# Group norm of a Mamba-2 branch on one core: sums in four column strips, roots as rows, spread through DRAM

## The reference

```
def grouped_rmsnorm(y, g, n_groups):
    shp = y.shape
    yf = y.astype(jnp.float32).reshape(*shp[:-1], n_groups, shp[-1] // n_groups)
    yf = yf * lax.rsqrt(jnp.mean(yf * yf, axis=-1, keepdims=True) + EPS)
    return yf.reshape(shp) * g
...
    y = y.reshape(bsz, seqlen, SSD_D_INNER) * jax.nn.silu(z.astype(jnp.float32))
    return grouped_rmsnorm(y, norm_g, SSD_N_GROUPS).astype(z.dtype)
```

## Time and profile before

| | us |
|---|---|
| median of 3 runs | 1487.44 (1487.26 to 1487.52) |
| the profiled execution, its own time | 1488.37 |
| span in the profile | 1486.5 |
| PE busy | 1476.8 (99%) |
| POOL busy | 948.5 (64%) |
| DVE busy | 780.4 (52%) |
| ACT busy | 522.8 (35%) |

### The profile page before, as it was taken

The page is one execution under the profiler, slowest core; times in us unless marked ns, Lnnn a source line. Parts: engine busy times, 40 slices in busy tenths (PEclk is TensorE's granted clock), DMA queues, the critical chain, the costliest instruction groups (busy, mean ns, idle before and its releaser), DMA issues.

```text
span 1486.5 us, 22863 instructions
## 1 busy us (share of the span) xinstructions
PE 1476.8 (99%) x8090; PEld 1211.9 (82%) x8090; DVE 780.4 (52%) x1084; ACT 522.8 (35%) x935; POOL 948.5 (64%) x945
## 2 busy tenths in 40 slices
PE   9999999999999999999999999999999999999999
PEld 7788878888787888888988888888888888888887
DVE  3556675566566648322655545500276483745723
ACT  4481551362263121111622222200242554636441
POOL 5356657665765789898167777799326564655544
PEclk9999999999999999999999999999999999999999
DMA  9244433533633344635022223234223222221231
GB/s 378 84 137 135 135 100 127 170 113 113 191 106 113 113 142 157 131 124 193 21 89 95 99 99 99 99 128 142 71 96 130 80 75 71 71 76 65 77 122 71
DMA packets 67982, 172.31 MB, mean 116 GB/s; under 512 B 7728, under 2 KB 24496, under 8 KB 66384
## 3 DMA queue, kind: packets, MB, share of 16 engines
q1 hardware_dynamic: 45504, 150.05, 30.5%
q10 hardware_dynamic: 22416, 21.44, 4.7%
HBM read 167.20 MB, written 4.27 MB: 115 GB/s over the span
## 4 chain that ended last, share of the span: by engine, by line
PE 97%; DVE 1%; DMA 1%; ACT 1%; issue 0%; SPq 0%; DVEq 0%; ACTq 0%
PE ps L611 17%; PE ps L614 17%; PE ps L613 17%; PE ps L628 6%; PE ps L630 5%; PE ps L629 5%; PE ps L978 4%; PE ps L979 4%; PE ps L977 4%; PE ps L879 1%; PE ps L1165 1%; PE ps L1240 1%; PE ps L1241 1%; PE ps L1242 1%; PE ps L1004 1%; PE ps L1000 1%
## 5 line engine op out<-in xcount | busy, mean ns | idle before, releaser
L561 POOL TENSOR_SCALAR w_hi<-raw 128x512 fp32r<-128x512 f32 x386 | 257.4, 685 | 506.3 <-PE ps L614 243.2
L566 POOL TENSOR_TENSOR w_lo<-raw,w_hi 128x512 fp32r<-128x512 f32 x386 | 527.5, 1388 | 0.0
L611 PE MATMUL ps<-h_hi,w_hi 128*128 128x512 f32 x880 | 347.7, 395 | 0.4 <-ACT zs L1386 0.2
L614 PE MATMUL ps<-h_hi,w_lo 128*128 128x512 f32 x880 | 342.9, 390 | 0.0
L613 PE MATMUL ps<-h_lo,w_hi 128*128 128x512 f32 x880 | 342.8, 390 | 0.0
L611 PEld LDWEIGHTS ps<-h_hi,w_hi 128*128 128x128 f32 x880 | 165.2, 188 | 39.2 <-issue 6.1
L614 PEld LDWEIGHTS ps<-h_hi,w_lo 128*128 128x128 f32 x880 | 165.2, 188 | 34.9
L613 PEld LDWEIGHTS ps<-h_lo,w_hi 128*128 128x128 f32 x880 | 165.3, 188 | 34.3 <-issue 1.0
L628 PE MATMUL ps<-h_hi,w_hi 128*128 128x512 f32 x352 | 140.8, 400 | 0.0
L630 PE MATMUL ps<-h_hi,w_lo 128*128 128x512 f32 x352 | 137.4, 390 | 0.0
L629 PE MATMUL ps<-h_lo,w_hi 128*128 128x512 f32 x352 | 137.3, 390 | 0.0
(11 more groups left out here) (429 smaller groups left out, 2826.4 us busy)
## 6 DMA issues: line engine op xcount, KB each, us to landing
raw<-stream SPq DMA_DIRECT2D x231, 512.0 KB, 3.3
ada_raw<-ada SPq DMA_DIRECT2D x64, 256.0 KB, 3.6
ada<-ada_first SPq DMA_DIRECT2D x8, 1024.0 KB, 14.7
abc<-acs_dram ACTq DMA_DIRECT2D x16, 512.0 KB, 7.2
raw<-stream SPq DMA_DIRECT2D x8, 256.0 KB, 11.9
xr<-x_classes ACTq DMA_DIRECT2D x1, 2048.0 KB, 10.1
x_dram<-xr ACTq DMA_DIRECT2D x1, 2048.0 KB, 8.3
x_res<-x_dram ACTq DMA_DIRECT2D x2, 1024.0 KB, 8.5
```

Of the source, the lines that this page charges most:

```text
L561: nc.gpsimd.tensor_scalar(hi[:, w], raw[:, raw_slot, w], 1.0, 1.0, ALU.mult, ALU.mult).then_inc(split_hi, 1)
L566: ins = nc.gpsimd.tensor_tensor(lo[:, w], raw[:, raw_slot, w], hi[:, w].bitcast(F32), ALU.subtract)
L611: nc.tensor.matmul(ps[:, bank], hi[:, w], x_hi[:, k0 + k], start=start and k == 0, stop=False)
L614: mm = nc.tensor.matmul(ps[:, bank], lo[:, w], x_hi[:, k0 + k], start=False, stop=stop and k == tiles - 1)
```

## The change

The factor of each token takes another way. The sums come out as rows: four products with 32 columns of ones as the weights and 128 tokens of `sct` as the moving side, each into its own strip of 32 partitions of bank 4. ACT takes the root of 128 x 128 (each strip holds 32 equal rows) into a new tile `norm_rows`, now ahead of conv_silu(0); DVE inverts all of it. ACT then sends rows 0, 32, 64 and 96 to a DRAM tensor, waits until they have landed, and reads the 512 numbers back into `sct` on all partitions. DVE's `scale_y` waits for that and reads `sct` in place of the bank. The diagonals and the product with ones are gone, with the semaphores that went with them; `gate_steps` counts 15 steps a group in place of 16.

```diff
+        norm_rows = at("norm_rows", FREE + 138 * KB + 384, [P, P])
...
+        norm_dram = nc.dram_tensor("norm_dram", (NT, P), F32, kind="Internal").ap()
...
             def column_sums(g):
 
-                pe.wait_ge(gate_steps, 1 + 16 * g + 6)
+                pe.wait_ge(gate_steps, 1 + 15 * g + 6)
                 for c in range(NT):
-                    mm = nc.tensor.matmul(ps[:, 4, c:c + 1], sct[:, c * P:(c + 1) * P], ones[:, 0:1], start=True,
-                                          stop=True)
-                mm.then_inc(group_sum, 1)
-
-            def spread_roots(g):
-
-                pe.wait_ge(gate_steps, 1 + 16 * g + 8)
-                nc.tensor.matmul(ps[:, 4], ones[:], sct[:], start=True, stop=True).then_inc(group_sum, 1)
+                    mm = nc.tensor.matmul(ps[32 * c:32 * c + 32, 4, 0:P], ones[:, 0:32], sct[:, c * P:(c + 1) * P],
+                                          start=True, stop=True, skip_group_check=True)
+                mm.then_inc(norm_steps, 1)
...
                 bias_in(1)
+                if not first:
+                    roots(g - 1)
                 conv_silu(0)
                 if not first:
-                    roots(g - 1)
+                    spread_roots(g - 1)
                 bias_in(2)
...
             def roots(g):
-                act.wait_ge(group_sum, 2 * g + 1)
-                A(small[:, 8:12], ps[:, 4, 0:4], ACT.Sqrt, bias=eps[:, 0:1], scale=1.0 / S).then_inc(group_root, 1)
+                act.wait_ge(norm_steps, 2 * g + 1)
+                A(norm_rows[:], ps[:, 4, 0:P], ACT.Sqrt, bias=eps[:, 0:1], scale=1.0 / S).then_inc(norm_steps, 1)
+
+            def spread_roots(g):
+                act.wait_ge(gate_steps, 1 + 15 * g + 7)
+                act.dma_start(norm_dram, norm_rows[0:P:32]).then_inc(norm_moved, 16)
+                act.wait_ge(norm_moved, 32 * g + 16)
+                act.dma_start(sct[:], norm_dram.rearrange("c t -> (c t)").unsqueeze(0).broadcast_to([P, S])
+                              ).then_inc(norm_moved, 16)
...
                 if part == (0, 1):
                     roots(GROUPS - 1)
+                    spread_roots(GROUPS - 1)
...
             def invert_roots(g):
-                dve.wait_ge(group_root, 1 + g + 1)
-                V.reciprocal(small[:, 12:16], small[:, 8:12]).then_inc(gate_steps, 1)
-                dve.wait_ge(gate_steps, 1 + 16 * g + 7)
-                TT(sct[:].rearrange("p (c t) -> p c t", c=NT), ident.unsqueeze(1).broadcast_to([P, NT, P]),
-                   small[:, 12:16].unsqueeze(2).broadcast_to([P, NT, P]), ALU.mult).then_inc(gate_steps, 1)
+                dve.wait_ge(norm_steps, 2 * g + 2)
+                V.reciprocal(norm_rows[:], norm_rows[:]).then_inc(gate_steps, 1)
 
             def scale_y(g):
-                dve.wait_ge(group_sum, 2 * g + 2)
+                dve.wait_ge(norm_moved, 32 * g + 32)
                 for b in range(4):
-                    STT(yg[:, b], yg[:, b], col("ssd_g", 4 * g + b), ps[:, 4], ALU.mult,
+                    STT(yg[:, b], yg[:, b], col("ssd_g", 4 * g + b), sct[:], ALU.mult,
                         ALU.mult).then_inc(gate_steps, 1)
```

More of the change, by code:

```diff
@@ L337, in build @@
         y_squared = sem("y_squared")
-        group_sum = sem("group_sum")
-        group_root = sem("group_root")
+        norm_steps = sem("norm_steps")
+        norm_moved = sem("norm_moved")
         y_hi_ready = sem("y_hi_ready")
@@ L401, in build @@
         out_stored = sem("out_stored")
-        start_at_one = [group_root, chunk_steps, state_steps, mod_ready, gate_steps, biased,
+        start_at_one = [chunk_steps, state_steps, mod_ready, gate_steps, biased,
                         pt_ready, decays, sc_steps, y_done, mix_steps, attended, ada_steps, units_done,
@@ L771, in column_sums @@
             def column_sums(g):
-                pe.wait_ge(gate_steps, 1 + 16 * g + 6)
+                pe.wait_ge(gate_steps, 1 + 15 * g + 6)
                 for c in range(NT):
-                    mm = nc.tensor.matmul(ps[:, 4, c:c + 1], sct[:, c * P:(c + 1) * P], ones[:, 0:1], start=True,
-                                          stop=True)
-                mm.then_inc(group_sum, 1)
-            def spread_roots(g):
-                pe.wait_ge(gate_steps, 1 + 16 * g + 8)
-                nc.tensor.matmul(ps[:, 4], ones[:], sct[:], start=True, stop=True).then_inc(group_sum, 1)
+                    mm = nc.tensor.matmul(ps[32 * c:32 * c + 32, 4, 0:P], ones[:, 0:32], sct[:, c * P:(c + 1) * P],
+                                          start=True, stop=True, skip_group_check=True)
+                mm.then_inc(norm_steps, 1)
             def y_half(u, slot, n, g, bank, free):
                 if n == 0:
-                    pe.wait_ge(gate_steps, 1 + 16 * g + 16)
+                    pe.wait_ge(gate_steps, 1 + 15 * g + 15)
                 unit(u, slot, bank, free, y_hi, y_lo, tiles=4, at_k=4 * (n % 2),
@@ L851, in turn @@
                         pe.wait_ge(dt_tokens, 1)
-                        pe.wait_ge(gate_steps, 1 + 16 * g)
+                        pe.wait_ge(gate_steps, 1 + 15 * g)
                     cols = slice(c * P, (c + 1) * P)
@@ L871, in outputs @@
                     pe.wait_ge(chunk_steps, 1 + 24 * g + 6 * c + 6)
-                    pe.wait_ge(gate_steps, 1 + 16 * g + max(c - 1, 0))
+                    pe.wait_ge(gate_steps, 1 + 15 * g + max(c - 1, 0))
                     if c:
@@ L892, in group @@
                     conv(2)
-                    spread_roots(g - 1)
                     conv(3)
@@ L943, in _ @@
                     column_sums(GROUPS - 1)
-                if i == 3:
-                    spread_roots(GROUPS - 1)
                 if i == 19:
@@ L1371, in conv_silu @@
                     if j == 2 and not first:
-                        act.wait_ge(gate_steps, 16 * g - 9)
+                        act.wait_ge(gate_steps, 15 * g - 8)
                     dst = (BT[:], CT[:])[j] if j < 2 else xcT[:, j - 2]
@@ L1377, in skips @@
                     act.wait_ge(conv_out, 6 * g + 6)
-                    act.wait_ge(gate_steps, 1 + 16 * g)
+                    act.wait_ge(gate_steps, 1 + 15 * g)
                     for b in range(4):
@@ L1407, in square @@
                 def square():
-                    act.wait_ge(gate_steps, 1 + 16 * g + 5)
+                    act.wait_ge(gate_steps, 1 + 15 * g + 5)
                     A(xcT[:], yg[:], ACT.Square).then_inc(y_squared, 1)
@@ L1479, in roots @@
             def roots(g):
-                act.wait_ge(group_sum, 2 * g + 1)
-                A(small[:, 8:12], ps[:, 4, 0:4], ACT.Sqrt, bias=eps[:, 0:1], scale=1.0 / S).then_inc(group_root, 1)
+                act.wait_ge(norm_steps, 2 * g + 1)
[6 more added lines that the diff above has]
+                              ).then_inc(norm_moved, 16)
             def y_his(g, bs):
                 for b in bs:
-                    act.wait_ge(gate_steps, 1 + 16 * g + 8 + b + 1)
+                    act.wait_ge(gate_steps, 1 + 15 * g + 7 + b + 1)
                     A(y_hi[:, b], yg[:, b], ACT.Copy).then_inc(y_hi_ready, 1)
@@ L1982, in gate @@
                 def gate():
-                    dve.wait_ge(gate_steps, 1 + 16 * g + 4)
+                    dve.wait_ge(gate_steps, 1 + 15 * g + 4)
                     dve.wait_ge(evacuated, E_GRP + 6 * g + 4)
```

## The result

The changed kernel takes **1503.41 us** (median of 4 runs, 1503.16 to 1504.39), the kernel before beside it 1487.48. The ratio is 1.0108, with a 95% interval of 1.0096 to 1.0119: slower by 15.9 us, where 1482.6 was forecast and 1481.8 to 1486.6 given as the range. The profiled execution took 1504.39 us with a span of 1502.6.

The account below looks back on a forecast made before the run. PE was taken to bound the touched part; its gain of 1.22 us per group, four times, gave 4.9 us with no new waits, so span 1481.6 and median 1482.6 us, range 1481.8 to 1486.6.

Parts of the forecast that it names:

- PE's part: Column sums and dropped product with ones on PE: gain of 1.22 us per group, four times, 4.9 us.
- The write: ACT's 2 KB write to DRAM in the first loop pass: 1.7 us to landing, 2.7 from above, ACT standing still.
- The read: 256 KB read back into sct in the first loop pass: 4.0 us, between 2.7 and 5.1.
- the page: Trainium skill's DMA rule, about 2.0 us plus bytes over 436 GB/s per transfer: 4.6 us for write and read.
- The start of scale_y: DVE in the first loop pass: scale_y starts at 160.0 instead of 159.48, as the read lands.
- the cover: Slack before PE waits at y(0): ends when scale_y starts at about 160.5, write and read together over 6.25 us.
- The price of meeting POOL: scale_y in the first loop pass: little slowdown beside POOL's one-operand passes, 0.82 us a pass; through by 162.9.
- rival 4: DVE and POOL shut each other out, 1.95 us a pass; last group 2.5 us late, 1485.1 us; chance 0.02.
- deadline: First loop pass: taps(3) with two y_lo must start by 164.1 for PE not to wait at y(0).
- The last group: Behind the loop: scale_y ends at 541.9, y_lo at 547.4, y projections start at 549.5, 2.1 us to spare.
- Rival 1: Round trip late in the loop: PE waits 3.3 us at y(0) in three passes, 1493.7 us; chance 0.08.
- Rival 2: Write and read take 6.4 to 7 us: 0.2 to 1.5 us a pass, 1483.2 to 1487.1 us; chance 0.14.

Follow-up runs that it names:

- PE's part alone: The changed kernel without the two transfers and their waits, and with scale_y reading PSUM bank 4 instead of sct: 1482.65 us.
- PE kept busy: The changed kernel with sixteen unread 128-column products into a free bank ahead of y(0) in each loop pass: 1497.66 us.

## Why the prediction was wrong, point by point

- **PE's part: right.** The last product ahead of the sums starts at 148.66, the second one behind them at 149.67: two beats and 0.56 us; 0.55 was said. PE's part alone gave 5.1 us, for 4.9.

```profile
148.97 0.43 PE L778 MATMUL ps<-sct,ones 128*32 128x128 f32 x8
```

- **The write: too short in the loop.** From issue to the read's issue it is 2.73 us (153.68 to 156.41), 2.82 and 2.66 in the other passes, where 1.7 was taken, the row of a 64 KB store. The bound from above, 2.7, was the value. In the last group the same write takes 1.61, so there 1.7 was right. The stretches of the first write and of the last differ in what else the DMA engines do, a busy share of 0.78 and of 0.04 (last column but one):

```profile
153.70:156.40 2.70, 2.70 (x14) 2.23 (x13) 0.52 (x1) 0.01 (x1) 1.24 (x3) 1.00 0.78 240
547.90:549.50 1.60, 1.60 (x8) 1.32 (x8) 1.60 (x1) 0.00 (x0) 0.47 (x1) 1.00 0.04 12
```

  That other traffic makes the write longer fits this; no run tests it by itself.
- **The read: too long.** With SyncE issuing, it goes out at 155.90 and scale_y starts on its landing at 159.18: 3.3 us at most (3.4 and 3.5 in the other passes), where 4.0 was taken. The pair takes 6.0 to 6.3 us for 5.7, so the sum of the two was nearly right, and nearer than the 4.6 us estimated from the page; what did harm in the change as it stood was their split, since the write's share is the time for which ACT stands.
- **The start of scale_y: late by 0.9 us.** The stop put bias_in(2) at 157.15, taps(2) at 158.09 and scale_y at 160.55. This pass began 0.38 us earlier than in the old trace (ACT's first table load at 143.84 for 144.22), so on the prediction's footing it is 160.9, past the 160.5 at which the text said the cover ends. The text held the late bias_in(2) to be harmless for PE's sake, and carried it to taps(2) at 157.4 (158.5 measured, on that footing).
- **The price of meeting POOL: the step that failed.** The text took 0.82 us for a DVE pass beside POOL's one-operand passes and a mean of 1.38 beside the rest, so that at most one pass in four would suffer: 2.9 us for scale_y, where 4.47 were measured (5.58 and 4.48 in the other passes). One by one, the passes read:

```profile
160.55 0.74 DVE L1904 SCALAR_TENSOR_TENSOR yg<-yg,tab,sct 128x512 f32<-128x512 f32 x1
160.60 1.17 POOL L564 TENSOR_SCALAR w_hi<-raw 128x512 fp32r<-128x512 f32 x1 [1.72 <-PE ps L617]
161.21 1.10 DVE L1904 SCALAR_TENSOR_TENSOR yg<-yg,tab,sct 128x512 f32<-128x512 f32 x1
161.74 1.05 POOL L564 TENSOR_SCALAR w_hi<-raw 128x512 fp32r<-128x512 f32 x1
162.23 1.09 DVE L1904 SCALAR_TENSOR_TENSOR yg<-yg,tab,sct 128x512 f32<-128x512 f32 x1
162.76 1.71 POOL L569 TENSOR_TENSOR w_lo<-raw,w_hi 128x512 fp32r<-128x512 f32 x1
163.25 1.77 DVE L1904 SCALAR_TENSOR_TENSOR yg<-yg,tab,sct 128x512 f32<-128x512 f32 x1
164.43 1.74 POOL L569 TENSOR_TENSOR w_lo<-raw,w_hi 128x512 fp32r<-128x512 f32 x1
```

  The first DVE pass begins ahead of POOL's and takes its own time. Then the starts alternate, one of DVE and one of POOL, and DVE's stand 1.02 us apart beside one-operand passes and 1.69 beside a two-operand pass. Alone a DVE pass takes 0.68 us, POOL's 0.60 and 1.27; strictly in turn they would give 1.28 and 1.95, so it is taking turns, with 0.26 us of overlap. The 1.38 of the earlier trace rows was the mean of the two kinds (twice 1.02 and twice 1.69 are 5.42, the row has 5.51), not a price that speaks against a lock. And the other row, read for DVE's 0.82 us alone, had the lock in its POOL half: two w_hi passes at 1.89 us where they take 1.21 alone, longer by 0.68, one DVE pass. There POOL paid. A later start of scale_y isn't needed for the miss: with SyncE issuing, the first pass starts it where the forecast had it (159.18, which is 160.1 after a shift of 0.93 by the second bias, for 160.0), and it takes 3.46 us there, for 2.9, and some 4.5 in the other two passes, where PE waits. So rival 4's mechanism was nearly the true one; it was given 0.02 and looked for only in the last group. The Trainium skill, "SBUF — State Buffer", section "SBUF: two separate sides", has it: the shared port pair is an exclusive lock when DVE has two SBUF inputs against a GpSimd pass that reads SBUF. The traces agree, with the PSUM operand too (2.71 us beside the split), except for the 0.26 us of overlap; the prediction set the page aside on a mean over unlike passes.
- **The chain behind it: not priced at all.** Of the 3.9 us by which y(0) is late, scale_y makes 1.2 (taps(3) start at 164.94 for a deadline of 164.1 - 0.38) and the two pairs of y_lo 3.15 (3.46 + 2.35 - 2 x 1.33); these are 4.35. That is more than 3.9 because PE itself has slipped: conv(5) was due at 165.79 by the beat and starts 0.5 us late, as POOL's slowed split isn't done, so that the beat behind it puts y(0) later too:

```profile
166.29 0.49 PE L614 MATMUL ps<-h_hi,w_hi 128*128 128x512 f32 x1 [0.34 <-POOL w_lo L569]
```

  In the trace of before each y_lo lay in a hole of POOL; a slower POOL has none, and each y_lo meets the next split.
- **The clock: not priced.** In the three passes y(0) is 3.90, 5.11 and 3.92 us late, 12.9 in all; the products behind it lose 2.66, 2.93 and 1.70 to the slower beat, 7.3; waits for POOL 0.6. That is 20.8 of the 21.4 us between the profiled executions of the change (1504.39) and of PE's part alone (1482.98). With PE kept busy the profiled execution was 7.8 us shorter, medians 5.75. The clock's two levels are 2.4 and 1.2 GHz; 512 columns in 0.427 us are the lower one. The Trainium skill, "TensorE: Matmul & The Clock Gate", Part 1, has such a gate, which halves the clock of an engine that has idled; the trace agrees, 0.88 behind the wait and 1.00 where PE was kept busy.
- **The last group: right that it is covered.** Scale_y waits 2.5 us for the read, takes 5.64 us for the 5.5 of the text, y_lo 5.51, and PE doesn't wait there.
- **The rivals.** Rival 1 had the place (y(0)) and the sign, with 0.08 of the chance, but got them from a late landing. That its wait of 3.3 us a pass lies near the 3.9, 5.1 and 3.9 measured is luck; without the clock its sum of 1493.7 stays 9.7 below the result. Rival 2 held the actual start of scale_y, 0.9 us late, though not by its way, and priced it at what it would be without feedback, 0.2 to 1.5 us a pass.

## What to carry to other kernels

Before an operand is moved from PSUM to SBUF, look at what GpSimd runs in the same microseconds. Here DVE passes with two SBUF operands and GpSimd's passes from SBUF went in turn. So price each DVE pass that meets one at its own time plus that of the GpSimd pass (0.26 us less here), kind by kind and never by a mean, read both engines' rows, and follow the loss to the next pair that lay in a hole until then. Waits of TensorE like these, 3.9 to 5.1 us, are to be priced with what the slower clock takes behind them, here 1.7 to 2.9 us more each. A round trip through DRAM is cheap only where it is issued early enough for every engine: moving the same step one unit ahead turned a loss of 15.9 us into a gain of 5.1.

## What the runs showed of the hardware that was not expected

- One-operand GpSimd passes (w_hi, 0.60 us alone) lock against a DVE pass with two SBUF operands too: 1.05 to 1.17 us for them and 1.10 for DVE's 0.68.
- A write of 2 KB to DRAM from four partitions holds its issuer for 2.7 to 2.8 us in the loop, more than the 1.7 us in which a store of 64 KB landed, and for 1.6 in the last group, where the DMA engines are nearly idle.
- The kernel in which the read's landing sets the start of scale_y, within a microsecond of the split, scatters by 8 us from run to run, where every other one keeps within 1.6. Why was not followed.
- TensorE's slower beat followed a shorter wait as well: with SyncE issuing, y(0) of the second pass starts at 298.62 behind 2.5 us of waiting, and its products stand 0.427 us apart from 299.51 to 302.07.
